# Two orders changed in a one-core transformer kernel: when ScalarE issues its first small loads, and when it splits the weights for the second chunk of the feed-forward stage

## What is computed

```
u = h @ w_in[i]                                   # first block, first thing done with x
...
u = rmsnorm(h, mlp_norm_g[layer])                 # second block, both layers
h = h + jnp.square(jax.nn.relu(u @ w_ff1[layer])) @ w_ff2[layer]     # width 1024 -> 4096 -> 1024
```

## Time and profile before

| what | value |
|---|---|
| time, median of 3 runs | 1948.29 us (1945.57 to 1949.42) |
| time of the profiled execution | 1949.42 us |
| its span, first to last instruction | 1947.6 us |
| PE busy | 1727.3 us, 89% |
| PE weight loads busy | 1201.4 us, 62% |
| DVE busy | 796.3 us, 41% |
| ACT busy | 482.6 us, 25% |
| mean granted PE clock | 0.935 |
| DMA | 347.03 MB, mean 178 GB/s |

### The profile page before, as it was taken

One profiled execution on the slowest core, in us unless ns is written; L12 is line 12 of the kernel. 1 busy time (PEld: TensorE's weight loads), 2 busy tenths in 40 slices (PEclk: granted clock), 3 DMA queues, 4 the chain that ended last, 5 costly groups with the idle time before them and its releaser, 6 DMA issues.

```text
span 1947.6 us, 22595 instructions
## 1 busy us (share of the span) xinstructions
PE 1727.3 (89%) x9115; PEld 1201.4 (62%) x9115; DVE 796.3 (41%) x1726; ACT 482.6 (25%) x894; POOL 0.5 (0%) x7
## 2 busy tenths in 40 slices
PE   7958999898895899999879986586899999899998
PEld 6644444343574544434347555586689995469998
DVE  7882411000404331100045455655355553726655
ACT  1142111010214211101022341111144442325443
POOL 0000000000000000000000000000000000000000
PEclk9968999999996899999999867697999999999999
DMA  9061489999706058999962000000434443303541
GB/s 309 1 237 38 171 312 391 396 392 367 252 0 237 9 188 309 392 396 392 385 239 87 1 1 1 0 1 1 173 130 173 173 172 134 125 1 111 192 172 65
DMA packets 153353, 347.03 MB, mean 178 GB/s; under 512 B 8240, under 2 KB 15280, under 8 KB 153280
## 3 DMA queue, kind: packets, MB, share of 16 engines
q1 hardware_dynamic: 145904, 338.28, 47.0%
q10 hardware_dynamic: 7376, 7.74, 1.4%
HBM read 344.96 MB, written 1.05 MB: 178 GB/s over the span
## 4 chain that ended last, share of the span: by engine, by line
PE 75%; DMA 9%; DVE 9%; ACT 3%; issue 2%; SPq 2%; DVEq 0%; ACTq 0%
PE ps L718 72%; DMA ring<-in_w_up 8%; DVE ring L1826 3%; SPq L624 2%; DVE arena L1826 1%; PE ps L1094 1%; PE ps L725 1%; DVE ring L1832 1%; DMA ring<-in_w_in 1%; DVE small L1994 0%; ACT hT L1394 0%; ACT arena L1394 0%; DVE ring L1829 0%; PE ps L811 0%; DVE small L2236 0%
## 5 line engine op out<-in xcount | busy, mean ns | idle before, releaser
L718 PE MATMUL ps<-ring,arena 128*64 128x512 f32 (+6 forms) x1728 | 388.2, 585 | 28.3 <-DMA ring<-in_w_up 17.8
L718 PEld LDWEIGHTS ps<-ring,arena 128*64 128x64 f32 (+2 forms) x1728 | 141.4, 146 | 257.6 <-issue 250.6
L718 PE MATMUL ps<-arena_r,ring_r 128*128 128x272 f32 (+1 forms) x1024 | 291.0, 284 | 0.0
L1394 ACT ACTIVATE arena<-ps 128x512 f32<-128x512 f32 (+7 forms) x179 | 79.9, 475 | 536.9 <-PE ps L718 328.1
L718 PEld LDWEIGHTS ps<-arena_r,ring_r 128*128 128x128 f32 x1024 | 192.5, 188 | 0.0
L718 PE MATMUL ps<-arena_r,ff_hi_r 128*128 128x272 f32 (+1 forms) x992 | 186.2, 285 | 2.8 <-DVE hT L1826 2.8
L718 PE MATMUL ps<-ring,hT 128*128 128x512 f32 (+2 forms) x448 | 180.1, 561 | 8.1 <-DMA ring<-in_w_in 2.6
L718 PE MATMUL ps<-ring 128*128 128x128 f32 (+2 forms) x848 | 133.6, 326 | 37.7 <-DVE ring L1826 30.3
L718 PEld LDWEIGHTS ps<-arena_r,ff_hi_r 128*128 128x128 f32 x992 | 154.8, 189 | 3.2 <-DVE hT L1826 3.2
L718 PE MATMUL ps<-arena_r,y_r 128*128 128x272 f32 (+1 forms) x544 | 149.0, 286 | 6.8 <-issue 3.0
L718 PE MATMUL ps<-arena 128*128 128x512 f32 (+9 forms) x420 | 121.3, 487 | 35.9 <-DVE small L1829 18.0
(11 more groups left out here) (282 smaller groups left out, 1860.2 us busy)
## 6 DMA issues: line engine op xcount, KB each, us to landing
ring<-in_w_down SPq DMA_DIRECT2D x32, 2048.0 KB, 14.5
ring<-in_w_gate SPq DMA_DIRECT2D x32, 2048.0 KB, 17.5
ring<-in_w_up SPq DMA_DIRECT2D x32, 2048.0 KB, 19.2
ring<-in_w_ff SPq DMA_DIRECT2D x32, 2048.0 KB, 8.6
ring<-in_w_in SPq DMA_DIRECT2D x8, 2048.0 KB, 18.6
ring<-in_w_in_ab SPq DMA_DIRECT2D x5, 2048.0 KB, 12.9
ring<-in_w_o SPq DMA_DIRECT2D x4, 2048.0 KB, 11.7
ring<-in_ple_gate SPq DMA_DIRECT2D x4, 2048.0 KB, 19.8
```

The source lines that it names most:

```text
L718: return pe.matmul(o, lhsT, rhs, start=a, stop=z)
L1394: return act.activation(o, i, ACT.Copy, scale=scale)
```

## The change

Two things move, and no instruction is added or removed. First, the twelve small DMAs that ACT issued behind `feature_major(0)` are issued ahead of it, right behind the first four. Second, on ACT and on DVE the splitting of units 4 and 5 moves behind `squares_of_relu(0, 0)`, where the first step now does it like every other step. This is in `feed_forward(L)`, and so happens once in each of the two layers. PE's and SP's programs are the same.

```diff
+            load_prm(0)
+            load_ln(0)
+            act.wait_ge(setup_done, 1)
+
+            act.dma_start(ln_cols, A["ln_cols"]).then_inc(ln_cols_load, 16)
+            act.dma_start(fm, A["feature_par"]).then_inc(const2_load, 16)
+            act.wait_ge(pad_zero, 1)
+            act.dma_start(h[0:N_META, NT, :], A["meta"]).then_inc(const2_load, 16)
 
             for l in range(DEPTH):
                 if l == 0:
-                    act.wait_ge(setup_done, 1)
                     feature_major(0)
-                    load_prm(0)
-                    load_ln(0)
-                    act.dma_start(ln_cols, A["ln_cols"]).then_inc(ln_cols_load, 16)
-                    act.dma_start(fm, A["feature_par"]).then_inc(const2_load, 16)
-                    act.wait_ge(pad_zero, 1)
-                    act.dma_start(h[0:N_META, NT, :], A["meta"]).then_inc(const2_load, 16)
...
@@ ACT, feed_forward(L)
-                for U, m, dd, q, ahead in ff_units(L, 0, 0, False)[:2]:
-                    high_part(U, m, dd, q, ahead)
                 squares_of_relu(0, 0)
 
                 def step(j, d, first=False, last=False):
-                    for U, n, dd, q, ahead in ff_units(L, j, d, last)[2 if first else 0:]:
+                    for U, n, dd, q, ahead in ff_units(L, j, d, last):
                         high_part(U, n, dd, q, j + ahead)
...
@@ DVE, feed_forward(L)
-                for U, n, dd, q, ahead in ff_units(L, 0, 0, False)[:2]:
-                    low_part(U, n, dd, q)
                 squares_of_relu(0, 0)
 
                 def step(j, d, first=False, last=False):
-                    for U, n, dd, q, ahead in ff_units(L, j, d, last)[2 if first else 0:]:
+                    for U, n, dd, q, ahead in ff_units(L, j, d, last):
```

## The result

The changed kernel takes 1969.0 us (median of 4 runs, 1967.23 to 1971.13), the kernel before 1948.53 beside it (1945.57 to 1949.42). The ratio is 1.0108, with an interval of 1.0096 to 1.0121: slower by 20.5 us where the forecast was 11.7, and outside the range. The direction and the place of the feed-forward part were right. The start was not: it was forecast to cost 0.75 us.

The account below looks back on a forecast made before the run. PE was taken to bound the kernel, with 75% of the chain. Feed-forward pauses 7.5, clock 3.4 and start 0.75 us summed to 11.7 us, giving 1960.0 us on the median of 1948.29; range 1955.0 to 1965.0.

Parts of the forecast that it names:

- The start: Before PE's first projection matmul: the moved DMAs delay the landing of `w_in` slot 0 by 0.75 us.
- The pause in the feed-forward stages: At unit 4 in each stage, PE waits longer for DVE's low part: 3.8 and 3.7 us, together 7.5.
- The clock: Behind each new feed-forward pause PE runs 3.4 us at half clock, losing 1.7 us; 3.4 us for both.
- The feed-forward sum: Both feed-forward stages together: 7.5 us of longer pauses and 3.4 us of half clock.
- upper bound of 3.8: At the start: 1.55 MB of moved loads at 411 GB/s all come before slot 0, costing 3.8 us.
- Only the last 1.5 us of slot 0's transfer has them beside it for certain.: At the start: the moved DMAs queue behind the bias, landing at 13.1; half of the 1.5 us was taken.
- 3.7 us are covered there: Second `w_in` slot: landed at 23.7, PE through with slot 0 at 27.4, so 3.7 us of lateness is covered.
- the twelve would end at 8.7: At the start: ACT issues the twelve DMAs in 5.6 us, ending at 8.7, before its wait for PE ends at 9.61.
- The delay of PE's start isn't caught up: First attention, after the projections: DVE waits 7.0 us for PE, so PE's late start carries through.
- More loss: Rival: 6.8 us half clock in both stages, 1963.4 us, or slot 0 behind all ACT's loads, 1963.1; chance 0.18.
- Faster: Rival, clock throughout the kernel: seven fewer half-clock stretches of 1.7 us each give 1948.1 us; chance 0.02.
- not late: Rival, feed-forward stages: the moved splitting delays nothing, only 0.75 us stays, 1949.0 us; chance 0.03.

Follow-up runs that it names:

- ff_only: The kernel before with only the splitting of units 4 and 5 moved behind the squares on ACT and DVE; 1962.12 us, ratio 1.0068.
- ff_fill5: ff_only with PE doing five matmuls on constants, computing nothing, in the pause of each feed-forward stage; 1960.75 us, ratio 1.0056.
- start_only: The kernel before with only ACT's twelve DMAs moved ahead of `feature_major(0)`; 1954.36 us, ratio 1.0032.
- start_prm: The kernel before with only the seven small parameter-row DMAs (0.35 MB) moved ahead of `feature_major(0)`; 1956.0 us, ratio 1.0029.
- start_dve_hT: start_only with the four copies into hT made by DVE and not ACT; 1955.91 us, ratio 1.0027.
- start_fewer: The kernel before with the positions and relative bias DMAs also issued behind `feature_major(0)`; 1950.09 us, ratio 1.0006.

## Why the prediction was wrong, point by point

- **The pause in the feed-forward stages** was right in place, cause and size. Forecast 3.8 and 3.7 us more on DVE's low part of unit 4; measured 4.3 (5.55 against 1.25) and 3.8 (5.00 against 1.20). The half microsecond in the first is DVE's wait of 0.46 us between its two operations of the squares. It is there in ff_only too, not in the second stage, and the copied durations of the earlier trace rows did not have it; no run explains it. "The delay is neither repeated nor given back" held: PE has no other wait in the stages that it did not have before, and ff_fill5's stages are longer by the pause alone. Moving the work away brought nothing, as said.
- **The clock** was right in kind and too small: "the shortest that the rows show", 3.4 us, was taken, and both stretches lasted 6.8 us, 5.6 of it over PE's work. Forecast 1.7 us each; ff_only against ff_fill5 gives 2.2 and 2.4. The reason that was given for the short one (dense work follows) is refuted: dense work did follow here. The rival with 6.8 us counted 3.4 each, too much: a stretch begins 1.2 us before PE does.
- **The feed-forward sum** was 10.9 us; measured in after's trace 6.85 + 6.29 = 13.1, and 13.3 (10.7 to 15.8) by ff_only.
- **The start is the step that failed**, in size: "I take half of the 1.5 us, 0.75 us"; it is 6.35 us in after's trace and 6.2 (3.9 to 8.6) by start_only's ratio, where start_only's own trace has 3.77. So it is at least five times the term, and at or above the upper bound of 3.8. PE's first projection matmul alone moved by 3.29 us, past the 3 us that the prediction named as its sign of being wrong. Three of the prediction's statements here were false, and two terms were missing.
  - "Only the last 1.5 us of slot 0's transfer has them beside it for certain." The rule of turns was cited and then applied to the last piece alone. The relative bias ends q10's work of before (22 packets are left at 12.0 us, none at 13.1); with twelve DMAs behind it the queue isn't empty before slot 0 has landed, and slot 0's queue gets a third of the bytes that it had. Of the 405 packets that this queue has fewer from 12.0 to 14.6 us, 295 follow from equal turns and 110 from the unexplained fall of the total. The bound of 3.8 us was made from bytes at full rate, and start_prm shows bytes not to be the price: 0.35 MB cost 3.05 us.
  - The next slot's "3.7 us are covered there". It lands at 31.8, 8.1 us later than before, while ACT's loads are in flight until 31.3 us (the meta tokens, issued at 13.10, took 18.2). 3.3 of the 8.1 are slot 0's delay, behind which it stands. From 17 to 23 us the queues take equal turns in both kernels (758 and 749 packets before, 545 and 549 after), so what differs there is again the total, and its cause is open. PE waits for this slot 2.13 us after having started late.
  - ACT's issues "fit": "the twelve would end at 8.7". They ended at 14.50. start_dve_hT and start_prm show this not to be what costs, since slot 0 is as late without it. Counted alone it would have held PE to nearly the same time (17.87).
  - The sum had no term for the clock at the start, and none for a second slot that is late.
- **"The delay of PE's start isn't caught up"** was right in the first attention, where DVE's wait of 7.0 became 12.0, and for start_only, whose 3.77 us are 4.53 at the start of the first feed-forward stage. In after's execution 2.5 of its 6.35 us were gone by there. What I did not say is that the 7.0 us is a cover in the other direction too, which is what start_fewer ran into.
- **The rivals.** "More loss" named both true mechanisms, the longer half clock and slot 0 behind ACT's loads, but as alternatives of one size, 3.1 and 3.4 us. Both came, and the second was 5.6 us above the forecast's term in after's trace, not 3.1. "Faster" and "not late" did not come.
- **The range** left out that the start's bound had been made for PE's first wait alone, without the second slot and without the clock behind a longer pause.

## What to carry to other kernels

In this kernel a DMA that is issued early on another queue wasn't priced by its bytes. As long as that queue had anything left, it took every second packet beside a load that PE waited for, so ask until when it stays non-empty, and count the next slots as well as the first. Read the queue's packets in the window that ends with the critical landing: an empty second queue there is what the change would take away. And where work is moved out from under a wait, look at which engine must do it next and for how long PE stands, then add the clock behind the pause. The same holds for a load that is moved later: ask which engine needs it, and how long that engine's cover is.

## What the runs showed of the hardware that was not expected

- Two queues with work move packets in equal numbers (in after 406 and 409 from 8 to 11 us; 208 and 210 from 12.0 to 14.6). In the second window the total is 161 packets per us, against 244 in before with one queue at work, but in the first it is 272: the fall doesn't go with two queues as such.
- ACT's issue of a DMA took 0.33 to 0.58 us for each of the twelve in before. In after the five that follow the seven parameter rows took 1.0 to 2.2 us each. In start_prm none of the seven rows, alone ahead of the copies into hT, took over 0.67 us, and of the five issued behind the copies the second took 1.62. What sets the longer issues no run isolates.
- Pauses of 5.55 and 5.00 us in PE's work were each accompanied by 6.8 us at 0.50, which began 1.2 us before PE restarted. With fillers in the same place, leaving gaps of 1.26 and 0.70 us, the clock stayed at 1.00.
- At the start, behind a wait of 2.63 us, the first ten matmuls of the first group took 0.59 us each and the later ones 0.30; behind a wait of 1.27 us (start_fewer) none was slow. So part of what an earlier slot 0 gives is the pace behind a shorter wait.
